# Two attention blocks on one Trainium2 core: a later place in the queues for exponentials and divisions, and an output tile begun inside the last stick-breaking pair

## The chip, the cores and the metric

The kernel runs on one core of one Trainium2 chip. The metric is the device time of one execution in microseconds (us). The core has five engines that each work through a queue of their own in program order: TensorE (PE in the profile, its weight loads PEld), VectorE (DVE), ScalarE (ACT), GpSimd (POOL) and SyncE (SP). They meet only at semaphores: an instruction carries `then_inc`, and another engine's queue stops at `wait_ge`.

## The reference, cut to what matters

The program is two transformer blocks one after the other, on 1024 positions of width 1024, in float32. The change touches two places.

The sparse attention of the first block: every query picks 256 keys by an index score, and six heads in two groups attend to those. The kernel computes full logits and masks them.

```
logits = jnp.einsum('bqgrd,bqkgd->bqgrk', qg, k_sel).astype(jnp.float32) * att_scale
logits = jnp.where(valid[:, :, None, None, :], logits, -jnp.inf)
p = jax.nn.softmax(logits, axis=-1).astype(v.dtype)
o = jnp.einsum('bqgrk,bqkgd->bqgrd', p, v_sel)
```

The stick-breaking attention of the second block (12 heads of 64) and the projection that follows it:

```
log_stay = jnp.where(strict, jax.nn.log_sigmoid(-z), 0.0)
later = lax.cumsum(log_stay, axis=3, reverse=True) - log_stay
w = jnp.where(strict, jnp.exp(jax.nn.log_sigmoid(z) + later), 0.0)
...
y = jnp.concatenate([mix, mem_out.astype(mix.dtype)], axis=-1) @ w_out[layer]
x = layer_norm(DN_ALPHA * x + y, ln_mix_g[layer], ln_mix_b[layer])
```

## The kernel before

Everything stands in one program with the order of every engine's work written out by hand. A float32 product is made of three TensorE passes: each operand is split into a rounded high part and a low part (the difference), and high*high, high*low and low*high are added. So each weight tile of 128x1024 is split by GpSimd (`split`, L467 the high part, L469 the low part) into `w_hi` and `w_lo`, two slots each, and the split of tile t waits until tile t-2 has been used (`tile_done` at t-1). A tile of the big products is 8 blocks of 6 matmuls of 512 columns (L558, L559, L562), and writes one of the two slots of the PSUM tensor `dense`.

The sparse attention. `DSA_PLAN` lists 16 pairs (query block i of 128, group g), called s. Each has 3 heads, so that n = 3s+j counts 48 strips of logits of width 128(i+1). `DSA_TURNS` lists, for each s, its i+1 key blocks: 72 steps x. At step x TensorE turns three 128x128 pieces of the probabilities (`att_turn`, L870), may make logits for a later n (`att_logits`, L858 and L859; `LOGITS_AT` says at which x), and multiplies with the values of step x-2 (`att_values`, L880). The logits of s are made during the steps of s-2, and their turn comes two s later. ScalarE at step x copies the turned piece to SBUF (L1301); then rounds the queries of a later s, where `QUERIES_AT` says so (L1232, once for each s); then takes the exponentials (L1288) of the strips whose logits are made at this same x. VectorE at step x takes the low part of those queries (`split_queries`, L1775, which waits for the rounding), turns the index score into a mask when a new i begins (L1834), adds the mask to the logits and finds the extreme of each row (`mask`, L1839), and divides the strips of step x-1 (`normalise`, L1846 and L1848). TensorE may turn piece x only when the copy of piece x-2 has been made; it may make logits n only when `mask` of n-2 is done.

The stick-breaking attention. 12 heads of 12 steps n (144 in all), two heads are a pair of 24 steps. At step n TensorE makes scores (L1004 to L1006), turns the weights of step n-6 (`turn_weights`, L1016) and multiplies those of step n-8 with the values (`values`, L1030 and L1031), and in all pairs but the last adds a piece of the next pair's projections (L978 to L980). ScalarE takes two sigmoids (L1473, L1479) and rounds the turned weights (L1487). VectorE scans the row (L2060; in the third kind of step a one-column product, L2059, stands before it), and takes the low part of the turned weights (L2067). GpSimd multiplies weights and scan (`stick_steps`, L517) and, at 12 steps of a pair, splits a half of a weight tile (L500, L507). In the last pair (steps 120 to 143) the finished attention output `y2_f` is prepared for the projection: at the steps of `EARLY_AT` (130, 132, ... 142) ScalarE rounds one of 7 blocks of it (L1501) and VectorE takes its low part (`low`, L1638). The eighth block is finished only after the last step.

After the last step TensorE waits for the last head (`y_copied`) and runs `two_tiles`: output tiles `T_OUT2` and `T_OUT2+1` woven together, the second four blocks behind the first. GpSimd splits the weights of `T_OUT2+2` when the first of these two is done. VectorE adds each finished tile to the residual (L2089).

Of the kernel before, what the change touches and what calls it, by code (L numbers as in the profile page):

```python
# [20 lines left out]
F32 = mybir.dt.float32  # L21
F32R = mybir.dt.float32r
ACT = mybir.ActivationFunctionType
ALU = mybir.AluOpType
# [5 lines left out]
KB = D // P  # L30
# [8 lines left out]
SB_H = 12  # L39
# [40 lines left out]
U_OUT2 = U_SB  # L80
# [71 lines left out]
EARLY = 7  # L152
EARLY_AT = {PAIR_STEPS * (SB_H // 2 - 1) + 10 + 2 * j: j for j in range(EARLY)}

# [49 lines left out]
def build(nc, io, out):  # L204
    with ExitStack() as ctx:
# [5 lines left out]
        def sem(name):  # L211
            return ctx.enter_context(nc.semaphore(name))
# [74 lines left out]
        def par(name, k=0):  # L287
# [36 lines left out]
            "h", "mem", "ym", "yc", "ya", "merged", "h2", "hidden", "x2", "mem2", "y2", "x3", "hidden2")}  # L324
        yc_ready = sem("conv_out_ready")

        turned, roped, turn_free = sem("proj_turned"), sem("proj_rotated"), pair("turn_free")
# [136 lines left out]
        def _(pool):  # L464
# [48 lines left out]
            def stick_steps():  # L513
                for n in range(STICK_STEPS):
# [4 lines left out]
                    if n in SPLIT_W:  # L519
                        t, part = SPLIT_W[n]  # L520
                        split_part(T_SB + t, part)

            split_tiles(RAW, T_ATT + 2)
# [18 lines left out]
        def _(pe):  # L542
# [496 lines left out]
            for n in range(STICK_STEPS + PV_LAG):  # L1039
# [9 lines left out]
                if n in TURN_V:  # L1049
                    turn_values(*TURN_V[n])  # L1050

            pe.wait_ge(v_split, SB_H)
            pe.wait_ge(y_copied, 2 * SB_H)
            for n in range(KB):
                if n == 0:
                    two_tiles(T_OUT2, U_OUT2, parts["y2"][1], Y2_ORDER)
                elif 2 <= n < KB - 2:
                    tile(T_OUT2 + n, U_OUT2 + n)
            last_two(3, T_OUT2 + KB - 2, U_OUT2 + KB - 2, lambda h: moments(3, h, U_OUT2))
# [26 lines left out]
        def _(act):  # L1086
# [209 lines left out]
            for x in range(len(DSA_TURNS) + DSA_LAG + 1):  # L1296
# [7 lines left out]
                if x in QUERIES_AT:  # L1304
                    round_queries(QUERIES_AT[x])
                for n in LOGITS_AT.get(x, ()):
                    exponentials(n)
# [249 lines left out]
        def _(dve):  # L1557
# [292 lines left out]
            for n in range(REP * DSA_LEAD + 2):  # L1850
                if n < REP * DSA_LEAD:
                    mask(n)
                if n >= 2:
                    normalise(n - 2)
            for x in range(len(DSA_TURNS)):
                if x in QUERIES_AT:
                    split_queries(QUERIES_AT[x])
                for n in LOGITS_AT.get(x, ()):
                    mask(n)
                for n in LOGITS_AT.get(x - 1, ()):  # L1860
                    normalise(n)

# [180 lines left out]
            for n in range(STICK_STEPS + PV_LAG + 1):  # L2043
# [31 lines left out]
                if n in EARLY_AT:  # L2075
                    j = EARLY_AT[n]
                    k = Y2_ORDER[j]
                    low((a_hi[:, k, :], a_lo[:, k, :]), k, y2_f[:, k, :], "y2", j + 1)

# [274 lines left out]
```

## Time and profile before

| | us |
|---|---|
| median of the timed runs (3) | 3115.48 (3112.72 to 3116.6) |
| the profiled execution, its own time | 3111.55 |
| its span in the profile | 3109.8 |
| sparse attention, first logits to last low part | about 726 to 868 |
| stick-breaking attention, last pair and tail | about 2200 to 2256.5 |
| the two woven output tiles | 2256.55 to 2278.41 |

The page counts busy time by engine over the span: PE 93%, PEld 75%, DVE 54%, ACT 25%, POOL 37%. Its 40 slices are 77.7 us each; the sparse attention lies in slices 10 and 11 and the end of the stick-breaking attention in slices 28 to 30. Averages over the span say little of either place: both are short, and each has its own limit.

### The profile page before, as it was taken

To read this page: it belongs to the slowest core of one execution; us is meant where nothing else is said; L and a number is where in the kernel's file an instruction comes from. 1 tells how busy PE (TensorE), PEld (TensorE's weight loads), DVE (VectorE), ACT (ScalarE), POOL (GpSimd) and SP (SyncE) were. 2 spreads that over 40 slices of the span, in tenths; PEclk is the share of its full clock that TensorE was granted. 3 is DMA by queue.
4 is the path that set the end of the run, shared out by engine and by line. 5 is a ranking of instruction groups with operands and counts; after the bars stand their busy time and mean duration, and the time that the engine had idled before them with its cause. 6 is when DMAs were issued, how large, how long until landed. Compare 5 with 4: busy or idle time off the path is not lost.

```text
span 3109.8 us, 34850 instructions
## 1 busy us (share of the span) xinstructions
PE 2907.6 (93%) x13074; PEld 2347.0 (75%) x13074; DVE 1689.6 (54%) x2299; ACT 789.0 (25%) x1441; POOL 1160.1 (37%) x649
## 2 busy tenths in 40 slices
PE   7987999998899999999999889999798999999997
PEld 5675878886577788888888668878585888888885
DVE  3475899987554423233232638888846233333327
ACT  4055011114622201011020456666613000000003
POOL 2330334442033334333333416555432344433331
PEclk9978999998999999999999999999898999999998
DMA  3110122221051111111111110000020111111111
GB/s 146 41 34 7 48 68 77 79 81 61 1 190 41 41 48 48 47 48 53 47 47 48 62 74 28 21 28 26 16 95 28 48 48 47 47 47 53 48 47 61
DMA packets 45051, 165.37 MB, mean 53 GB/s; under 512 B 4880, under 2 KB 6160, under 8 KB 43920
## 3 DMA queue, kind: packets, MB, share of 16 engines
q1 hardware_dynamic: 37168, 129.31, 12.5%
q10 hardware_dynamic: 7776, 34.61, 2.9%
q8 instruction: 70, 1.15, 0.2%
q14 instruction: 37, 0.30, 0.0%
HBM read 147.12 MB, written 16.78 MB: 53 GB/s over the span
## 4 chain that ended last, share of the span: by engine, by line
PE 80%; DVE 12%; ACT 3%; issue 3%; DVEq 1%; DMA 0%; POOL 0%; ACTq 0%; SPq 0%; POOLq 0%
PE dense L558 21%; PE dense L559 21%; PE dense L562 21%; DVE stay L2060 2%; DVE a_lo L1638 2%; PE dense L978 2%; PE dense L979 2%; PE dense L980 2%; PE dense L598 1%; PE dense L599 1%; PE dense L600 1%; PE side L1016 1%; ACT T L1198 1%; PE side L1005 1%; DVE T L1617 1%
## 5 line engine op out<-in xcount | busy, mean ns | idle before, releaser
L467 POOL TENSOR_TENSOR w_hi<-raw,zero 128x1024 fp32r<-128x1024 f32 x210 | 400.8, 1909 | 1565.6 <-PE dense L562 1298.7
L558 PE MATMUL dense<-a_hi,w_hi 128*128 128x512 f32 x2000 | 783.6, 392 | 14.1 <-DVE T L1791 5.6
L559 PE MATMUL dense<-a_lo,w_hi 128*128 128x512 f32 x2000 | 780.3, 390 | 0.0
L562 PE MATMUL dense<-a_hi,w_lo 128*128 128x512 f32 x2000 | 617.5, 390 | 0.0
L469 POOL TENSOR_TENSOR w_lo<-raw,w_hi 128x1024 fp32r<-128x1024 f32 x210 | 526.1, 2505 | 16.5
L558 PEld LDWEIGHTS dense<-a_hi,w_hi 128*128 128x128 f32 x2000 | 377.0, 188 | 95.8 <-issue 7.7
L559 PEld LDWEIGHTS dense<-a_lo,w_hi 128*128 128x128 f32 x2000 | 376.8, 188 | 79.2 <-issue 1.2
L562 PEld LDWEIGHTS dense<-a_hi,w_lo 128*128 128x128 f32 x2000 | 376.6, 188 | 78.5
L558 PE MATMUL dense<-b_hi,w_hi 128*128 128x512 f32 x832 | 327.2, 393 | 5.2 <-DVE T L1966 2.5
L559 PE MATMUL dense<-b_lo,w_hi 128*128 128x512 f32 x832 | 324.7, 390 | 0.0
L1946 DVE TENSOR_TENSOR x_res<-x_res,dense 128x1024 f32<-128x1024 f32 x100 | 122.0, 1220 | 329.6 <-PE dense L562 328.3
L1966 DVE SCALAR_TENSOR_TENSOR T<-dense,tiny,T 128x1023 f32<-128x1023 f32 x88 | 112.9, 1282 | 296.3 <-ACT T L1370 293.0
L562 PE MATMUL dense<-b_hi,w_lo 128*128 128x512 f32 x832 | 256.8, 390 | 0.0
L517 POOL TENSOR_TENSOR stick_weights<-stick_weights,stay 128x511 f32<-128x511 f32 (+2 forms) x144 | 132.2, 919 | 174.6 <-DVE stay L2060 174.6
L558 PEld LDWEIGHTS dense<-b_hi,w_hi 128*128 128x128 f32 x832 | 156.7, 188 | 45.7 <-issue 4.8
L1530 ACT ACTIVATE b_hi<-T 128x1024 fp32r<-128x1024 f32 x32 | 34.0, 1062 | 610.7 <-DVE T L2139 610.7
L562 PEld LDWEIGHTS dense<-b_hi,w_lo 128*128 128x128 f32 x832 | 156.5, 188 | 32.9
L559 PEld LDWEIGHTS dense<-b_lo,w_hi 128*128 128x128 f32 x832 | 156.8, 188 | 31.9
L1370 ACT ACTIVATE T<-dense,tiny 128x1024 f32<-128x1024 f32 x44 | 49.2, 1117 | 516.9 <-PE dense L562 511.1
L1742 DVE MATCH_REPLACE8 score<-tiny,score 128x384 f32<-128x384 f32 (+2 forms) x192 | 165.7, 876 | 0.0
L1738 DVE MAX8 tiny<-score 128x8 f32<-128x384 f32 (+2 forms) x192 | 155.4, 877 | 2.9 <-issue 1.6
L2137 DVE TENSOR_SCALAR T<-dense 128x1024 f32<-128x1024 f32 x32 | 39.2, 1225 | 192.1 <-PE dense L562 190.5
(277 smaller groups left out, 4360.0 us busy)
## 6 DMA issues: line engine op xcount, KB each, us to landing
raw<-in_w_stream SPq DMA_DIRECT2D x231, 512.0 KB, 3.3
x_in<-in_x_t SPq DMA_DIRECT2D x8, 512.0 KB, 7.4
spill_gate<-T ACTq DMA_DIRECT2D x8, 512.0 KB, 2.6
spill_part<-gates ACTq DMA_DIRECT2D x8, 512.0 KB, 2.6
back<-spill_gate ACTq DMA_DIRECT2D x8, 512.0 KB, 3.7
back<-spill_part ACTq DMA_DIRECT2D x8, 512.0 KB, 4.6
x_res<-in_x_t ACTq DMA_DIRECT2D x2, 2048.0 KB, 9.0
spill_x<-x_res ACTq DMA_DIRECT2D x1, 4096.0 KB, 13.4
```

Source lines behind the costliest of these rows:

```text
L467: pool.tensor_tensor(w_hi[:, r % 2, :], raw[:, r, :], zero[:, 0:1].broadcast_to([P, D]), ALU.add).then_inc(weights_rounded, 1)
L469: pool.tensor_tensor(w_lo[:, r % 2, :], raw[:, r, :], w_hi[:, r % 2, :].bitcast(F32), ALU.subtract).then_inc(weights_split, 1)
L517: pool.tensor_tensor(w[:, 0:width - 1], w[:, 0:width - 1], stay[n % STRIPS][:, 1:width], ALU.mult).then_inc(w_ready, 1)
L558: pe.matmul(o, w_hi[:, slot, w], hi[:, k, x], start=b == 0, stop=False)
L559: pe.matmul(o, w_hi[:, slot, w], lo[:, k, x], start=False, stop=False)
L562: last = pe.matmul(o, w_lo[:, slot, w], hi[:, k, x], start=False, stop=stop)
L978: pe.matmul(o, w_hi[:, t % 2, w], a_hi[:, b, x], start=b == 0, stop=False)
L979: pe.matmul(o, w_hi[:, t % 2, w], a_lo[:, b, x], start=False, stop=False)
L1738: dve.max(best[:, i - TOPK // P, :], score[:, score_at(i):score_at(i + 1)])
L1742: dve.match_replace(sc, best[:, i - TOPK // P, :], sc, TAKEN)
L1946: dve.tensor_tensor(x_res[:, n, :], x_res[:, n, :], dense[:, u % 2, :], ALU.add).then_inc(sums_free[u % 2], 1)
L1966: last = dve.scalar_tensor_tensor(T[:, slot, d:S], dense[:, u % 2, 0:S - d], tap, T[:, slot, d:S], ALU.mult, ALU.add)
```

## The change

In the sparse attention, ScalarE takes the exponentials one step later (those of x-1 at step x, behind the copy and the rounding of x). VectorE's step becomes: mask, divide the strips of x-2 (before x-1), and last the low part of the queries (before: first).

In the last stick-breaking pair, the 7 early blocks of `y2_f` are rounded three steps earlier (steps 127, 129, ... 139). The low parts of blocks j = 0, 2, 4, 6 move from VectorE to GpSimd; VectorE keeps 1, 3 and 5. Nine steps after each, TensorE multiplies the block for the output tile `T_OUT2+1` (at steps 136, 138, ... 148). After the last head, TensorE runs 7 blocks of tile `T_OUT2`, and then the eighth block of both.

```diff
-EARLY_AT = {PAIR_STEPS * (SB_H // 2 - 1) + 10 + 2 * j: j for j in range(EARLY)}
+EARLY_AT = {PAIR_STEPS * (SB_H // 2 - 1) + 7 + 2 * j: j for j in range(EARLY)}
+FIRST_AT = {n + 9: j for n, j in EARLY_AT.items()}
...
# GpSimd, stick_steps
+                    if n in EARLY_AT and EARLY_AT[n] % 2 == 0:
+                        j, k = EARLY_AT[n], Y2_ORDER[EARLY_AT[n]]
+                        pool.wait_ge(parts["y2"][0], j + 1)
+                        pool.tensor_tensor(a_lo[:, k, :], y2_f[:, k, :], a_hi[:, k, :].bitcast(F32), ALU.subtract
+                                           ).then_inc(y2_low, 1)
...
# TensorE, loop over the stick-breaking steps and what follows
-
-            pe.wait_ge(v_split, SB_H)
+                if n in FIRST_AT:
+                    j = FIRST_AT[n]
+                    if j == 0:
+                        pe.wait_ge(v_split, SB_H)
+                        pe.wait_ge(weights_split, T_OUT2 + 2)
+                    pe.wait_ge(parts["y2"][1] if j % 2 else y2_low, j // 2 + 1)
+                    product((T_OUT2 + 1) % 2, halves(dense, (U_OUT2 + 1) % 2), a_hi, a_lo, j + 1, begin=j, end=False, order=Y2_ORDER)
+
             pe.wait_ge(y_copied, 2 * SB_H)
-            for n in range(KB):
-                if n == 0:
-                    two_tiles(T_OUT2, U_OUT2, parts["y2"][1], Y2_ORDER)
-                elif 2 <= n < KB - 2:
-                    tile(T_OUT2 + n, U_OUT2 + n)
+            product(T_OUT2 % 2, halves(dense, U_OUT2 % 2), a_hi, a_lo, EARLY, end=False, order=Y2_ORDER)
+            pe.wait_ge(parts["y2"][1], KB // 2)
+            for n in range(2):
+                product((T_OUT2 + n) % 2, halves(dense, (U_OUT2 + n) % 2), a_hi, a_lo, KB, begin=EARLY, order=Y2_ORDER
+                        ).then_inc(tile_done, 1)
+            for n in range(2, KB - 2):
+                tile(T_OUT2 + n, U_OUT2 + n)
...
# ScalarE, sparse attention
-                for n in LOGITS_AT.get(x, ()):
+                for n in LOGITS_AT.get(x - 1, ()):
                     exponentials(n)
...
# VectorE, sparse attention
             for x in range(len(DSA_TURNS)):
+                for n in LOGITS_AT.get(x, ()):
+                    mask(n)
+                for n in LOGITS_AT.get(x - 2, ()):
+                    normalise(n)
                 if x in QUERIES_AT:
                     split_queries(QUERIES_AT[x])
-                for n in LOGITS_AT.get(x, ()):
-                    mask(n)
-                for n in LOGITS_AT.get(x - 1, ()):
-                    normalise(n)
...
# VectorE, stick-breaking
-                    low((a_hi[:, k, :], a_lo[:, k, :]), k, y2_f[:, k, :], "y2", j + 1)
+                    if j % 2:
+                        low((a_hi[:, k, :], a_lo[:, k, :]), k, y2_f[:, k, :], "y2", j + 1)
```

## Rows read from the trace of the kernel before

**Rows 1.** The page: span.

```profile
span 3109.8 us, 34850 instructions
```

**Rows 2.** Busy time by stretch: us, PE, PEld, DVE, ACT, POOL, PEclk (granted clock), DMA.

```profile
737.20:763.90 26.70, 21.56 (x91) 15.27 (x89) 17.53 (x61) 19.06 (x50) 2.02 (x2) 0.84 0.22 80
763.90:837.30 73.40, 58.21 (x263) 39.41 (x262) 42.18 (x95) 43.97 (x95) 4.01 (x4) 0.93 0.00 1
```

**Rows 3.** Waits from 763.9 to 837.3: who waited for whom, us, times, longest.

```profile
ACT strip L1288 <- DVE tiny L1839: 28.2, 18, 2.8
...
PE dense L870 <- ACT att_probs_t L1301: 15.2, 9, 3.2
DVE qq L1775 <- ACT qq L1232: 14.6, 7, 3.0
```

**Rows 4.** Timeline around step 29: start, us, engine, line, operation, idle before.

```profile
799.26 0.52 ACT L1232 ACTIVATE qq<-q_f 64x384 fp32r<-64x384 f32 x1
...
799.81 0.56 DVE L1775 SCALAR_TENSOR_TENSOR qq<-q_f,qq 64x384 fp32r<-64x384 f32 x1 [2.02 <-ACT qq L1232]
...
801.21 1.09 DVE L1839 CUSTOM_DVE_ANT_0 strip<-side,score 128x896 f32<-128x896 f32 x1 [0.18 <-issue]
...
802.34 1.04 ACT L1288 ACTIVATE strip<-strip,tiny 128x896 f32<-128x896 f32 x1 [2.56 <-DVE tiny L1839]
...
803.29 0.18 ACT L1288 ACTIVATION_READ_ACCUMULATOR strip<-strip,tiny 128x1 f32 x1
...
803.91 0.47 PE L870 MATMUL dense<-ident,strip 128*128 128x128 f32 x1 [2.60 <-ACT att_probs_t L1301]
```

**Rows 5.** Timeline of ACT where no logits are left: first and last of 11 copies.

```profile
854.01 0.49 ACT L1301 ACTIVATE att_probs_t<-dense 128x384 f32<-128x384 f32 x1 [0.47 <-PE dense L870]
...
863.76 0.49 ACT L1301 ACTIVATE att_probs_t<-dense 128x384 f32<-128x384 f32 x1 [0.48 <-PE dense L870]
```

**Rows 6.** Timeline of PE: turns before and after one strip, 640 and 1024 wide.

```profile
769.45 0.49 PE L870 MATMUL dense<-ident,strip 128*128 128x128 f32 x3
...
771.11 0.49 PE L870 MATMUL dense<-ident,strip 128*128 128x128 f32 x3
...
835.86 0.49 PE L870 MATMUL dense<-ident,strip 128*128 128x128 f32 x3
...
837.76 0.49 PE L870 MATMUL dense<-ident,strip 128*128 128x128 f32 x3
```

**Rows 7.** Busy time by stretch: last pair from scan 128 to 143; the two tiles.

```profile
2204.20:2244.80 40.60, 22.66 (x106) 17.71 (x106) 40.57 (x52) 26.84 (x55) 19.19 (x18) 0.78 0.04 14
2256.50:2278.40 21.90, 21.85 (x96) 18.13 (x97) 2.45 (x2) 2.12 (x2) 4.30 (x2) 1.00 0.52 204
```

**Rows 8.** Timeline of DVE: scan 128 alone, scan 130 beside a GpSimd pass.

```profile
2203.05 1.28 DVE L2060 TENSOR_TENSOR_SCAN stay<-stay,stay,zero 128x512 f32<-128x512 f32 x1
...
2208.81 2.38 DVE L2060 TENSOR_TENSOR_SCAN stay<-stay,stay,zero 128x512 f32<-128x512 f32 x1
```

**Rows 9.** Timeline of POOL: the passes beside scan 130; a whole weight split.

```profile
2207.79 1.09 POOL L517 TENSOR_TENSOR stick_weights<-stick_weights,stay 128x511 f32<-128x511 f32 x1 [1.29 <-DVE stay L2060]
2208.83 1.28 POOL L507 TENSOR_TENSOR w_lo<-raw,w_hi 128x512 fp32r<-128x512 f32 x1
...
2271.86 1.90 POOL L467 TENSOR_TENSOR w_hi<-raw,zero 128x1024 fp32r<-128x1024 f32 x1 [25.94 <-PE dense L562]
2273.83 2.40 POOL L469 TENSOR_TENSOR w_lo<-raw,w_hi 128x1024 fp32r<-128x1024 f32 x1
```

**Rows 10.** Groups of DVE from 2200 to 2250: busy us, mean ns; the eighth low part.

```profile
L1638 DVE TENSOR_TENSOR a_lo<-y_f,a_hi 128x1024 fp32r<-128x1024 f32 x7 | 11.8, 1690 | 0.0
...
2258.44 1.23 DVE L1638 TENSOR_TENSOR a_lo<-y_f,a_hi 128x1024 fp32r<-128x1024 f32 x1 [1.99 <-ACT a_hi L1507]
```

**Rows 11.** Timeline of PE: first product of the two tiles; first of the third.

```profile
2256.55 0.47 PE L558 MATMUL dense<-a_hi,w_hi 128*128 128x512 f32 x1 [1.45 <-issue]
...
2278.41 0.39 PE L558 MATMUL dense<-a_hi,w_hi 128*128 128x512 f32 x1
```

More of the change, by code:

```diff
@@ L325, in build @@
         yc_ready = sem("conv_out_ready")
+        y2_low = sem("y2_split_by_pool")
         turned, roped, turn_free = sem("proj_turned"), sem("proj_rotated"), pair("turn_free")
```

## The prediction

> **What bounds the kernel now.** I first read the page: the span is 3109.8 us [rows 1], and TensorE is busy for most of it, so a change counts only where TensorE stands idle or runs at the lower clock. Two stretches of the timeline belong to the change, and I read each by busy time, then by waits, then row by row.
>
> The sparse attention. From step 11 (its low part of the queries, L1775, starts at 763.9) to step 48 (its mask starts at 837.3) TensorE is busy for 58.2 of 73.4 us and its granted clock is 0.93, so a part of it ran at 1.2 GHz instead of 2.4 [rows 2]. The list of waits gives all of the 15.2 us of idleness to one wait: TensorE's turn (L870) waits for ScalarE's copy (L1301). ScalarE in its turn stood 28.2 us before its exponentials, waiting for VectorE's mask, and VectorE stood 14.6 us waiting for the rounded queries of ScalarE [rows 3]. Around step 29 the chain can be read link by link: ScalarE rounds the queries at 799.26, VectorE takes their low part at 799.81, then masks at 801.21, ScalarE's exponentials start at 802.34 after 2.56 us of idleness, its copies come behind, and TensorE's next turn starts at 803.91 after 2.60 us [rows 4]. The copies that TensorE wants are queued behind an exponential that is not ready.
>
> What would be left without these waits: a bare step lasts 9.75/10 = 0.975 us, from eleven copies in the tail of the stage [rows 5]. One strip of logits adds 1.66 - 0.975 = 0.69 us where it is 640 wide and 1.90 - 0.975 = 0.93 us where it is 1024 wide [rows 6]; for the 21 strips of steps 11 to 47, of 640 to 1024, I take the middle, 0.80. That makes 37 x 0.975 + 21 x 0.80 = 52.9 us for TensorE at its full clock. The stretch has 73.4, so 20.5 us are to be had: 15.2 of waiting, and 5 of lower clock, which agrees with 7% of 73.4.
>
> The end of the stick-breaking attention. From scan 128 to scan 143 VectorE is busy for 40.57 of 40.6 us [rows 7]: it is the bound, and TensorE has 18 us of room at a granted clock of 0.78. Then the two woven output tiles keep TensorE full for 21.86 us [rows 7, 11].
>
> **The change part by part: sparse attention.** Nothing is added or removed here, only the order changes. (1) ScalarE copies x+1 before it takes the exponentials of x, so the mask (1.09 us) has a whole step to finish; the wait of 28.2 us mostly goes. (2) VectorE masks before it waits for the queries, so L1775 and the ScalarE rounding leave the chain: 0.52 + 0.56 us and the mask of the score at each of the 12 rounds. (3) The division comes one step later. It is wanted only about one s later (4 steps or more from s = 6 on), so I cost it at nothing; what hides it is the lead of two s of the logits. (4) `split_queries` is now queued behind a mask and up to three divisions; TensorE wants it at the first strip of the next s, 4 to 6 steps on, but only 1 to 3 steps on before step 11. No DMA moves past anything: ScalarE's two fetches keep their place ahead of the exponentials.
>
> What is late next: not VectorE (42.2 us busy in 73.4) nor ScalarE (44.0), both under TensorE's 52.9 [rows 2]. But ScalarE at 44.0 of 52.9 is 83% full, and an exponential with its accumulator read (1.04 + 0.18 us, [rows 4]) still stands between two copies, so some waits remain. I take 16 of the 20.5 us, bounds 7 and 20. For steps 1 to 11 (737.2 to 763.9) TensorE is idle for 5.1 of 26.7 us at clock 0.84 [rows 2]; VectorE has many short strips there and becomes the bound, and (4) works against the gain: I take 2, bounds -3 and 6. For steps 48 to 54 I take 1. Sum: 19 us.
>
> **The change part by part: last stick-breaking pair.** (a) VectorE loses four low parts. In place they lasted 1.69 us on average, alone 1.23 [rows 10]; the difference is waiting for GpSimd, which the next scan would have to do as well. So VectorE is relieved of 4 x 1.2 = 4.8 us.
>
> (b) GpSimd gets four passes of the same kind as L469 over 1024 columns: 2.40 us each [rows 9], 9.6 us in all, and GpSimd has 21 us of room there [rows 7]. But the room is not what counts. Scan 128 lasts 1.28 us with GpSimd still; scan 130 lasts 2.38 us [rows 8], and in the second GpSimd's low-part pass began at 2208.83 and ended at 2210.11 [rows 9]: 2210.11 + 1.08 = 2211.19 is where the scan ends. The scan, which has its operands in SBUF, waited out the whole GpSimd pass. So the two engines take turns, and every pass moved to GpSimd is time in which VectorE's chain of scans stands still: +9.6. What VectorE does from PSUM (L2067, L2049) can run beneath, but that already runs beneath GpSimd's product L517, which goes first in the queue. So (a) and (b) make the last scan 9.6 - 4.8 = 4.8 us later; I take +5. Bounds: -6.8 (the passes cost VectorE nothing, all four of 1.69 are saved) and +9.6 (nothing is saved).
>
> The Trainium skill, "SBUF — State Buffer", section "SBUF: two separate sides", says the same against this change: the port pair of VectorE and GpSimd is a lock held for a whole instruction, and a VectorE instruction with two SBUF inputs waits for a GpSimd one that reads SBUF. By it the pair gets longer; by VectorE's busy time alone it would get 6.8 us shorter.
>
> (c) ScalarE's seven roundings only move three steps forward; it has 13 us of room [rows 7]. (d) TensorE's seven pieces of tile `T_OUT2+1`, 21.86/16 = 1.37 us each [rows 11], go into the pair. Four of them (steps 136 to 142) fall into gaps that wait for VectorE, and three into the tail, where they stand between turned weights but also keep the clock up (0.78 now); I cost them at nothing, bounds -1.5 and +4. Their operands are nine steps old, and the waits for them end no later than the ones TensorE has at that step anyway.
>
> (e) After the last head, TensorE had 16 pieces before tile `T_OUT2+2`, and now 9: 9.6 us less. (f) But the weights of `T_OUT2+2` may be split only when `T_OUT2` is done. Now this happens when 8 pieces are done, with one piece (1.37 us) left to cover GpSimd's 1.90 + 2.40 + 0.2 = 4.5 us [rows 9]; before, 4 to 5 pieces of the second tile covered it. TensorE stands 3.1 us. The eighth block's low part ends at 2259.67 [rows 10], 3.1 us after the first product, beneath the first seven pieces: nothing. So (e) and (f) give -9.6 + 3.1 = -6.5.
>
> Sum of the place: +5 - 6.5 = -1.5 us. Over both places: -19 - 1.5 = -20.5. The profiled execution took 3111.55 us, 1.75 more than its span, and would take 3091; the median of the runs lies 3.9 above it, so I predict 3115.5 - 20.5 = 3095.
>
> **The rivals.** (R1) ScalarE becomes the limit at every strip: an exponential, its read and a copy, 1.04 + 0.18 + 0.49 = 1.7 us [rows 4, 5], against a step of 0.975, and TensorE's one turn of lead doesn't absorb it. Then 21 x 0.73 = 15 us of the 20.5 stay, the stage gives 5.5 + 2, and with the other place the time is 3106.5. For it: ScalarE is second busiest. Against: only 21 of 37 steps have a strip.
>
> (R2) VectorE doesn't wait for the moved passes, as they fall where it waits anyway. Then the last scan comes 6.8 us earlier and the place gives 13.3: 3083. Against: 40.57 of 40.6 us busy.
>
> (R3) R1, and the inserted pieces lie on the path: 7 x 1.37 = 9.6 us, so that (e) is void and (f) and +5 remain. -7.5 + 5 + 3.1 = +0.6: 3116.
>
> (R4, slower) The low part of the queries at the end of VectorE's step. If TensorE reaches the first strip of the next s before VectorE reaches that line, it stands through mask, division and low part, 1.09 + 0.9 + 0.56 = 2.5 us, at each of 12 rounds: +30, against 19, with -1.5: 3125. It decides from the point where VectorE runs behind TensorE by the distance between rounds; with the distances of 4 to 6 steps it doesn't, with those of 1 to 3 (five rounds, +12.5) it may, but that alone leaves a gain.
>
> **How the numbers follow.** Forecast 60%, R1 17%, R2 11%, R3 8%, R4 4%. The forecast's own range is 3088 to 3103 (16 may be 10 to 19, +5 may be 2 to 9). To leave out no more than 2 in 10 it is widened to R1 and R2's edge: 3084 to 3107. A measurement of this kernel can tell 0.2%, 6.2 us, from no change. Faster by more: forecast, R1, R2, 88%; within: R3, 8%; slower: R4, 4%.
>
> **What would show it.** Right: ScalarE's wait before L1288 falls from 28.2 to under 8 us in the same steps, TensorE's wait for L1301 from 15.2 to under 5, the granted clock rises to 1.0, and steps 11 to 48 last 57 us. In the pair, GpSimd's low parts last 2.4 to 3.5 us, scans beside them over 2 us, the last head ends some 5 us later counted from step 128, and TensorE stands about 3 us before tile `T_OUT2+2`. Wrong: a wait of TensorE for L1775 (R4), scans as long as before (R2), or the sparse stage shorter by less than 10 us (R1).

## The result, and the profile after

The changed kernel takes 3081.96 us (median of 4 runs, 3080.82 to 3083.52); the kernel before, timed beside it, 3116.04. The ratio is 0.9893 with the interval 0.9876 to 0.991: 34.1 us less, where 20.5 were forecast. The time lies 2 us below the range, whose lower end was 3084. The profiled executions are 29.5 us apart, 3111.55 and 3082.01; below it is said how much of the difference between 34.1 and 29.5 has a cause that the traces show.

The changed lines bear new numbers in the profile after: the exponential L1288 is now L1303, the copy L1301 is L1316, TensorE's turn L870 is L877, the mask L1839 is L1854, the division L1846 and L1848 are L1861 and L1863, the queries' low part L1775 is L1790, the scan L2060 is L2075, GpSimd's weight split L467 and L469 is L469 and L471, the products L558, L559 and L562 are L565, L566 and L569. New is GpSimd's low part, L527. In the kernels of the experiments these numbers can be a few lines off.

First the page of after, its span and TensorE's share, beside [rows 1]:

```profile
span 3080.2 us, 34848 instructions
## 1 busy us (share of the span) xinstructions
PE 2901.3 (94%) x13074; PEld 2345.6 (76%) x13074; DVE 1690.0 (55%) x2295; ACT 788.6 (26%) x1441; POOL 1174.0 (38%) x653
```

**The sparse attention.** Stretches are best cut at ScalarE's copies, one for each of the 72 steps, since these have the same number in every kernel. The busy time by stretch, with the columns of [rows 2], from the copy of step 0 to that of step 11 and from there to that of step 48; before, then after:

```profile
734.52:762.82 28.30, 21.37 (x85) 14.99 (x85) 19.67 (x69) 19.56 (x54) 2.02 (x2) 0.80 0.21 75
762.82:837.83 75.01, 59.82 (x271) 40.52 (x270) 42.71 (x96) 45.51 (x100) 4.01 (x4) 0.93 0.00 1
```

```profile
736.03:757.90 21.87, 19.80 (x85) 14.00 (x85) 18.72 (x67) 18.75 (x51) 2.02 (x2) 0.83 0.28 97
757.90:809.06 51.16, 51.16 (x265) 37.46 (x264) 43.26 (x97) 44.67 (x101) 4.21 (x4) 1.00 0.00 1
```

In steps 11 to 48 TensorE is busy for all of 51.16 us, at a granted clock of 1.00. Its own busy time fell too, from 59.82 us, for the same products. A part of that is clock: a granted clock of 0.93 over 75.01 us means that some of the matmuls ran at 1.2 GHz, and 0.07 x 75.01 = 5.3 us is my estimate of the most that it can have cost. The rest comes with the waits themselves, as a kernel below shows that has waits at the full clock. Steps 0 to 11 lost 6.4 us, steps 11 to 48 lost 23.85, and the 23 steps behind them 0.7 (25.93 and 25.20). That is 31.0 us. What is left of the waits of [rows 3], in the same steps of after (who waits for whom, us, times, longest):

```profile
...
ACT att_probs_t L1316 <- PE dense L877: 5.6, 9, 1.4
DVE strip L1854 <- PE side L866: 2.5, 6, 0.8
DVE tiny L1861 <- ACT strip L1303: 2.3, 3, 1.4
PEld dense L877 <- ACT att_probs_t L1316: 1.2, 3, 0.5
...
ACT strip L1303 <- DVE tiny L1854: 0.3, 2, 0.2
```

ScalarE's 28.2 us before its exponentials are 0.3, and TensorE's 15.2 us before its turns are gone; only its weight load still waits 1.2 us, without holding up a matmul. Among TensorE, ScalarE and VectorE the largest wait now goes the other way: ScalarE waits for TensorE. The same place as [rows 4], around step 29, read from the timeline of after (start, us, engine, line, operation, idle before):

```profile
781.73 0.96 DVE L1854 CUSTOM_DVE_ANT_0 strip<-side,score 128x768 f32<-128x768 f32 x1 [0.54 <-PE side L866]
...
782.17 0.49 PE L877 MATMUL dense<-ident,strip 128*128 128x128 f32 x3
...
782.70 0.49 ACT L1316 ACTIVATE att_probs_t<-dense 128x384 f32<-128x384 f32 x1 [0.48 <-PE dense L877]
...
783.76 0.94 ACT L1303 ACTIVATE strip<-strip,tiny 128x768 f32<-128x768 f32 x1
783.97 0.49 PE L877 MATMUL dense<-ident,strip 128*128 128x128 f32 x3
...
784.18 1.09 DVE L1854 CUSTOM_DVE_ANT_0 strip<-side,score 128x896 f32<-128x896 f32 x1 [0.18 <-issue]
...
784.94 0.49 PE L877 MATMUL dense<-ident,strip 128*128 128x128 f32 x3
...
785.32 1.04 ACT L1303 ACTIVATE strip<-strip,tiny 128x896 f32<-128x896 f32 x1 [0.15 <-DVE tiny L1854]
```

The exponential over 768 columns starts at 783.76 right behind ScalarE's earlier work; its mask had started at 781.73 and lasted 0.96 us, so it was done 1.1 us earlier; the turns follow one another at 1.80 us with a strip between (782.17 to 783.97) and at 0.97 us without (784.94).

**The last stick-breaking pair.** Here moments are told from the start of the first scan of the whole stage, 1866.75 before and 1837.21 after. "The last value" is the start of VectorE's last sum into `y_f` (L2049, now L2064), which the output tiles wait for. Scan 128 started at 336.30 before and at 338.61 after, scan 143 at 376.73 and 377.77, the last value came at 389.01 and 390.99 and the third output tile (`T_OUT2+2`) at 411.66 and 410.27. So the pair itself became 2.0 us longer and the products behind it 3.4 us shorter. After, at the first moved low part, GpSimd and then VectorE:

```profile
2173.51 2.36 POOL L527 TENSOR_TENSOR a_lo<-y_f,a_hi 128x1024 fp32r<-128x1024 f32 x1
```

```profile
2174.41 1.48 DVE L2074 TENSOR_TENSOR stick_weights<-stick_weights,stay 128x1 f32<-128x1 f32 x1 [0.42 <-ACT stay L1494]
2175.82 1.27 DVE L2075 TENSOR_TENSOR_SCAN stay<-stay,stay,zero 128x512 f32<-128x512 f32 x1
```

VectorE's product of a single column lasts 1.48 us, and it ends at 2175.89, when GpSimd's pass does (2173.51 + 2.36 = 2175.87). The last pass of the four does the same at the product before a later scan (1.86 us). Scan 128 is 2.3 us later than before. But that is not the price of GpSimd's pass. The same place in the kernel whose low parts are all on VectorE (below), where the product has no pass of GpSimd beside it:

```profile
2173.54 1.96 DVE L1648 TENSOR_TENSOR a_lo<-y_f,a_hi 128x1024 fp32r<-128x1024 f32 x1 [0.30 <-ACT a_hi L1511]
...
2176.25 0.16 DVE L2069 TENSOR_TENSOR stick_weights<-stick_weights,stay 128x1 f32<-128x1 f32 x1
2176.33 1.28 DVE L2070 TENSOR_TENSOR_SCAN stay<-stay,stay,zero 128x512 f32<-128x512 f32 x1
```

Here the product lasts 0.16 us, but VectorE's own low part stands ahead of it, and scan 128 starts at 338.24, only 0.4 us earlier than with GpSimd. So 1.9 of the 2.3 us come from taking the first low part three steps earlier, ahead of scan 128, on whichever engine.

TensorE behind the last value, and at the third tile:

```profile
2228.94 0.79 PE L565 MATMUL dense<-a_hi,w_hi 128*128 128x512 f32 x1 [1.40 <-DVE y_f L2064]
...
2247.48 0.47 PE L565 MATMUL dense<-a_hi,w_hi 128*128 128x512 f32 x1 [3.19 <-POOL w_lo L471]
```

and the busy time of the first 6 us behind the one gap and the first 10 behind the other:

```profile
2228.90:2234.90 6.00, 5.96 (x14) 4.71 (x15) 1.22 (x1) 1.06 (x1) 0.00 (x0) 0.50 0.90 351
2247.50:2257.50 10.00, 10.00 (x37) 8.10 (x38) 0.91 (x1) 0.00 (x0) 5.03 (x2) 0.83 0.33 107
```

In both the granted clock is at the lower level for some or all of the time: TensorE does 14 matmuls in 6 us, and 27 in the kernel that closes the gap (below). Here each gap costs twice, as idleness and as clock. The first gap is not new: it was 1.45 us long before [rows 11]. The second is.

### The profile page after: what moved, and what is told of

It is laid out like the page before. It is cut to its first block, busy times and chain, and to the rows that moved or that the text cites. A ratio compares the mean times of both kernels' runs of the same rounds, so it can differ in the third digit from the quotient of the medians.

```text
span 3080.2 us, 34848 instructions
## 1 busy us (share of the span) xinstructions
PE 2901.3 (94%) x13074; PEld 2345.6 (76%) x13074; DVE 1690.0 (55%) x2295; ACT 788.6 (26%) x1441; POOL 1174.0 (38%) x653
## 4 chain that ended last, share of the span: by engine, by line
PE 82%; DVE 11%; ACT 2%; issue 2%; POOL 1%; DVEq 1%; DMA 0%; ACTq 0%; SPq 0%; POOLq 0%
PE dense L565 21%; PE dense L566 21%; PE dense L569 21%; PE dense L985 2%; PE dense L986 2%; PE dense L987 2%; DVE stay L2075 2%; DVE a_lo L1653 2%; PE dense L605 1%; PE dense L606 1%; PE dense L607 1%; PE dense L887 1%; PE side L1023 1%; ACT T L1213 1%; PE side L1012 1%
## 5 line engine op out<-in xcount | busy, mean ns | idle before, releaser
L469 POOL TENSOR_TENSOR w_hi<-raw,zero 128x1024 fp32r<-128x1024 f32 x210 | 401.3, 1911 | 1565.8 <-PE dense L569 1298.3
L565 PE MATMUL dense<-a_hi,w_hi 128*128 128x512 f32 x2000 | 785.1, 393 | 17.2 <-DVE T L1806 5.6
L566 PE MATMUL dense<-a_lo,w_hi 128*128 128x512 f32 x2000 | 781.6, 391 | 0.0
L569 PE MATMUL dense<-a_hi,w_lo 128*128 128x512 f32 x2000 | 618.4, 391 | 0.0
L471 POOL TENSOR_TENSOR w_lo<-raw,w_hi 128x1024 fp32r<-128x1024 f32 x210 | 525.0, 2500 | 16.5
L565 PEld LDWEIGHTS dense<-a_hi,w_hi 128*128 128x128 f32 x2000 | 377.5, 189 | 99.6 <-issue 9.4
L566 PEld LDWEIGHTS dense<-a_lo,w_hi 128*128 128x128 f32 x2000 | 377.5, 189 | 79.0 <-issue 1.2
L569 PEld LDWEIGHTS dense<-a_hi,w_lo 128*128 128x128 f32 x2000 | 377.3, 189 | 79.2
L565 PE MATMUL dense<-b_hi,w_hi 128*128 128x512 f32 x832 | 327.2, 393 | 5.2 <-DVE T L1981 2.5
L566 PE MATMUL dense<-b_lo,w_hi 128*128 128x512 f32 x832 | 324.7, 390 | 0.0
L569 PE MATMUL dense<-b_hi,w_lo 128*128 128x512 f32 x832 | 256.7, 390 | 0.0
L565 PEld LDWEIGHTS dense<-b_hi,w_hi 128*128 128x128 f32 x832 | 156.7, 188 | 45.8 <-issue 4.9
L569 PEld LDWEIGHTS dense<-b_hi,w_lo 128*128 128x128 f32 x832 | 156.5, 188 | 32.9
L566 PEld LDWEIGHTS dense<-b_lo,w_hi 128*128 128x128 f32 x832 | 156.8, 188 | 31.7
```

The source lines that it names most:

```text
L469: pool.tensor_tensor(w_hi[:, r % 2, :], raw[:, r, :], zero[:, 0:1].broadcast_to([P, D]), ALU.add).then_inc(weights_rounded, 1)
L471: pool.tensor_tensor(w_lo[:, r % 2, :], raw[:, r, :], w_hi[:, r % 2, :].bitcast(F32), ALU.subtract).then_inc(weights_split, 1)
L565: pe.matmul(o, w_hi[:, slot, w], hi[:, k, x], start=b == 0, stop=False)
L566: pe.matmul(o, w_hi[:, slot, w], lo[:, k, x], start=False, stop=False)
L569: last = pe.matmul(o, w_lo[:, slot, w], hi[:, k, x], start=False, stop=stop)
```

## The experiments

Times are medians; "before" is always the kernel before, timed beside the kernel in question on the same chip. The kernels came in three groups, and before took 3115.91, 3115.2 and 3114.66 us in them (3116.04 beside the changed kernel), so a difference between kernels of different groups is uncertain by a microsecond or so.

**The two places apart.** The diff shown ahead of the prediction is cut in two. The first kernel has only this of it, and the old pair; the second has all the rest.

```diff
-                for n in LOGITS_AT.get(x, ()):
+                for n in LOGITS_AT.get(x - 1, ()):
                     exponentials(n)
...
+                for n in LOGITS_AT.get(x, ()):
+                    mask(n)
+                for n in LOGITS_AT.get(x - 2, ()):
+                    normalise(n)
                 if x in QUERIES_AT:
                     split_queries(QUERIES_AT[x])
```

> Only the order in the sparse attention is changed, the last stick-breaking pair is as before. Theory S (the whole gain of 34 us lies in the sparse attention, as the ledger of the two traces has it: 31 us there, 1.5 us of drift elsewhere): 3085 us, 30 to 32 below the kernel before. Rival (the sparse part is worth the 19 us that I forecast, and the rest comes from the pair): 3097 us.

Measured: 3084.88 us, ratio 0.9901 (0.9885 to 0.9918): -31.0 us, as the first theory has it. Steps 11 to 48 last 51.15 us, as in the changed kernel.

> Only the last stick-breaking pair and the output tiles are changed, the sparse attention is as before. Theory S: 0 to 2 us below the kernel before, since the head ends 2 us later, the tiles start 9.6 us shorter, and GpSimd's split and the lower clock take 3 us each. Rival: 12 to 15 us below.

Measured: 3111.46 us, ratio 0.9988 (0.9978 to 0.9997): -4.4 us. That is more than the 0 to 2 us expected, though the interval (0.9 to 6.9 us) reaches into them. Together the two kernels gain 35.4, beside the 34.1 of the whole change. So nine tenths come from the sparse attention, and the pair gains a little more than forecast, though its trace looks like a draw. The traces say in part why. From the first scan to the end of the span it is 1243.0 to 1243.1 us in all three kernels with the new pair and the early products (the changed one, the pair alone, and the changed one with doubled masks, below). With the old pair the profiled execution of before has 1243.0, but the five other kernels with the old pair have 1245.4 to 1245.5. They part behind the last value. Busy time of 7 us from there, of the kernel with the old pair and the new orders:

```profile
2223.70:2230.70 7.00, 6.98 (x24) 5.57 (x25) 1.23 (x1) 1.06 (x1) 0.00 (x0) 0.76 0.93 359
```

The granted clock is at 0.76 here, and in the other four as well, where it was 1.00 in the profiled execution of before [rows 7]. That execution was a favourable one; against the usual one the new pair is worth 2.5 us.

This explains a part of the difference between the two figures of the result. The profiled executions differ by 31.0 - 1.5 = 29.5: the three parts of the sparse attention gave 31.0, and the stage began 1.5 us later (its first copy at 736.03 and not 734.52; over the executions of all kernels that copy comes between 734.4 and 737.7). The medians differ by 4.5 us more, of which 2.5 are the favourable execution of before. The other 2 us are not explained. From the last copy of the sparse attention to the first scan, a stretch that no edit touches, the profiled executions take between 1000 and 1003.6 us, so a remainder of this size can't be given to any part of the change.

**Which order does it.** The first kernel moves only the exponentials, the second only the split of the queries, behind mask and division, and the third exponentials and divisions but not the split.

```diff
-                for n in LOGITS_AT.get(x, ()):
+                for n in LOGITS_AT.get(x - 1, ()):
                     exponentials(n)
```

> Only ScalarE's exponentials come one step later; VectorE keeps its old order. Theory Q (the round trip of the queries, ScalarE's rounding to VectorE's low part to the mask, is most of the wait): 8 to 14 us below the kernel before, since VectorE still waits for the rounding before it masks, but the exponentials no longer stand in front of the copy. Rival E (the place of the exponentials is all that counts): 27 us or more below.

```diff
-                if x in QUERIES_AT:
-                    split_queries(QUERIES_AT[x])
                 for n in LOGITS_AT.get(x, ()):
                     mask(n)
                 for n in LOGITS_AT.get(x - 1, ()):
                     normalise(n)
+                if x in QUERIES_AT:
+                    split_queries(QUERIES_AT[x])
```

> Only VectorE's order is changed: mask, then the division of the step before, then the low part of the queries; ScalarE keeps its old place for the exponentials. Theory Q: 8 to 14 us below the kernel before, as the query round trip leaves the chain, but every exponential still stands before the next copy and waits 1 us or more for its mask. Rival E: 3 us or less below.

```diff
-                for n in LOGITS_AT.get(x, ()):
+                for n in LOGITS_AT.get(x - 1, ()):
                     exponentials(n)
...
-                for n in LOGITS_AT.get(x - 1, ()):
+                for n in LOGITS_AT.get(x - 2, ()):
                     normalise(n)
```

> The kernel before with exponentials and divisions one step later, the split of the queries still ahead of the mask on VectorE; the stick-breaking pair is as before. With the exponentials alone later the 37 steps 11 to 48 took 56.5 us, with all three orders changed 51.2. If what is left there is the split's wait for ScalarE, which the mask behind it on VectorE inherits: 56 us again, 3090 to 3091 us. If it is the division that waits for an exponential issued in the same step: 51 to 52 us, 3085 to 3086 us.

Measured, with the parts of the stage in us:

| orders changed | time | less than before beside it | steps 0 to 11 | 11 to 48 | 48 to 71 |
|---|---|---|---|---|---|
| none | 3115.91 | | 28.30 | 75.01 | 25.93 |
| split last | 3094.85 | 21.1 | 23.61 | 59.92 | 25.93 |
| exponentials later | 3090.93 | 25.0 | 25.27 | 56.48 | 25.19 |
| exponentials and divisions later | 3088.37 | 26.3 | 25.55 | 53.25 | 25.20 |
| all three | 3084.88 | 31.0 | 21.42 | 51.15 | 25.21 |

Neither theory of the first two was right (8 to 14 us each, or 27 or more and 3 or less). The two edits don't halve the gain between them, nor does one have it all: each alone brings most of it, as both cut the same chain (queries rounded, their low part, mask, exponential, copy). With one link out, what is left fits nearly into a step. The waits of steps 11 to 48 with the split last:

```profile
ACT strip L1288 <- DVE tiny L1839: 13.6, 14, 1.7
...
PE dense L870 <- ACT att_probs_t L1301: 4.4, 6, 1.6
DVE qq L1775 <- ACT qq L1232: 1.2, 1, 1.2
```

and its busy time:

```profile
760.73:820.65 59.92, 55.34 (x271) 37.23 (x270) 42.47 (x96) 45.30 (x101) 4.01 (x4) 1.00 0.00 1
```

The granted clock of that stretch is 1.00, not 0.93, and yet TensorE is busy for 55.34 us, 4.2 more than in the changed kernel, for the same products. So with waits between the matmuls the trace counts more busy time at the full clock too, and of the 8.7 us that TensorE's busy time fell by (59.82 to 51.16) at most 4.5 are the clock's. With the exponentials later alone it is 9.0, 3.3 and 3.1 us for these, and 1.00 as well. The clock thus came back to 1.00 with either edit, before the waits were gone. The third kernel tells the rest apart. Taken in this order, the later division is worth 3.2 us in steps 11 to 48 (56.48 to 53.25), the split's place 2.1 more, and in steps 0 to 11 it is the split's place that counts, 25.55 to 21.42 (21.4 to 22.7 in all seven executions with these orders and no doubled mask). Its 53.25 us lie between what I gave for the one cause and for the other; both have a share, the division the larger.

**How much room the new order has.** Every fourth mask is done twice, in the changed kernel and in the one before.

```diff
+                if n % 4 == 1:
+                    dve.tensor_tensor_reduce(out=strip_of(n), ...)
+                    dve.drain()
                 dve.tensor_tensor_reduce(out=strip_of(n), ...)
```

> The changed kernel with every fourth mask of the sparse attention done twice on VectorE, about 1.0 us more work each time, five times in steps 11 to 48 and some more before. Slack theory (with the new order TensorE alone sets these steps, and VectorE's 43 of 51 us are off the path): steps 11 to 48 stay within 1 us of 51.2, and the time within 2 us of 3082. Chain theory (mask, exponential and division still follow one another within what a step lasts): 4 to 6 us more in these steps, 3087 to 3090 us.

> The kernel before with the same every fourth mask done twice. Chain theory for the order before (mask, exponential, its division and the next mask lie in one row, so that work on VectorE goes straight to the end): 4 to 6 us more in the 37 steps 11 to 48 than 75.0, and 3121 to 3124 us in all. If VectorE's waits there absorb it: 3116 us.

Measured: 3088.89 us (0.9916, 0.9899 to 0.9933), 6.9 over the changed kernel; and 3124.98 (1.0029, 1.0019 to 1.0038), 10.3 over before. VectorE's busy time over steps 0 to 71 rose by 8.4 us in both. In steps 11 to 48 it rose by 3.8 us in the new kernel (43.26 to 47.05) and the stretch by 3.3, to 54.48; in the old one by 5.0 and 5.5, to 80.54. My slack theory, with at most 1 us, falls. The chain theory had 4 to 6 us in these steps: in the new order it is a little less, and in the old one the time is 1 us above the 3121 to 3124 expected, with executions from 3118.5 to 3126.5. TensorE was full in these steps but the chain of mask, exponential and division stood right behind it: its waits are back at once, here those of steps 11 to 48 with the doubled masks in the new order.

```profile
ACT strip L1303 <- DVE tiny L1858: 6.4, 8, 1.7
...
PE dense L877 <- ACT att_probs_t L1316: 1.3, 2, 1.1
```

**The price of GpSimd's low parts.** All seven on VectorE, the rest as changed.

```diff
-                    pool.tensor_tensor(a_lo[:, k, :], y2_f[:, k, :], a_hi[:, k, :].bitcast(F32), ALU.subtract
-                                           ).then_inc(y2_low, 1)
...
# TensorE, for each early piece
-                    pe.wait_ge(parts["y2"][1] if j % 2 else y2_low, j // 2 + 1)
+                    pe.wait_ge(parts["y2"][1], j + 1)
...
-                    if j % 2:
-                        low((a_hi[:, k, :], a_lo[:, k, :]), k, y2_f[:, k, :], "y2", j + 1)
+                    low((a_hi[:, k, :], a_lo[:, k, :]), k, y2_f[:, k, :], "y2", j + 1)
```

> The changed kernel with all seven low parts of the output's input on VectorE, as before the change; the early products and the sparse attention's orders stay. Port theory (each GpSimd pass over 128x1024 numbers holds VectorE's scans for its whole 2.4 to 3.3 us, where VectorE's own pass takes 1.2): from the start of the stick-breaking attention to the end of scan 143 about 2 us less than in the changed kernel (whose scan 143 comes 1.9 us later than before), so 3080 us. Relief theory (four passes taken from VectorE are 4.8 us of its time saved): scan 143 later by up to 4.8 us, 3085 to 3087 us. If the head is bound by something else than VectorE: 3082 us, as the changed kernel.

Measured: 3082.11 us (0.9892, 0.9875 to 0.9908), by time the same as the changed kernel, where 3080 was expected. By the trace, scan 143 starts at 376.46 and the last value comes at 389.66, both 1.3 us earlier than in the changed kernel; in the six profiled kernels with the new pair and GpSimd's low parts scan 143 lies between 377.7 and 378.3. The relief theory is out: taking four passes of VectorE's away didn't shorten its chain, it lengthened it. The size is smaller than the forecast's 4.8, and the time alone couldn't have shown it; another pair of kernels does, below. The third tile starts 2.6 us earlier than in the changed kernel, but what follows it lasts 1.5 us longer, with the same granted clock of 0.83 in the first 10 us; why is not shown.

**The price of the early products.** Low parts on GpSimd, but both tiles multiplied after the last value.

```diff
-                if n in FIRST_AT:
-                    ...
-                    product(..., j + 1, begin=j, end=False, order=Y2_ORDER)
...
+            two_tiles(T_OUT2, U_OUT2, None, Y2_ORDER)
```

> The changed kernel with the four low parts on GpSimd, but both output tiles multiplied after the last values, as before the change. What it prices is moving seven of sixteen pieces of 1.36 us each ahead. Full theory (the move is worth its 9.5 us): 3091 us. Clock and stall theory (in the changed kernel the move is worth 9.5 us less 3.0 us for the granted clock of 0.50 after the gap of 1.4 us, and less 3.2 us for the stall ahead of the third tile, which comes with it): 3085 us, the granted clock in the first 10 us after the last values 1.00, and the stall ahead of the third tile under 1 us. Nothing theory (the products inserted in the pair cost the head what they save behind it): 3082 us.

Measured: 3083.46 us (0.9896, 0.988 to 0.9913; 3081.20 to 3087.53), 1.5 us over the changed kernel, where 3085 was expected. The executions spread over 6 us, and the profiled one is the longest, so its end proves little. Its moments do: the last value comes at 390.16, 0.8 us earlier than with the inserted products, and the third tile at 414.2, 3.9 us later. The 9.6 us of products moved ahead are thus worth 3.9 at that point. The granted clock behind the last value is 0.75, not the 1.00 I expected; there is no stall before the third tile, as expected.

**The gap behind the last value.** The seventh early piece is held back until the last product of the values is issued, so it fills TensorE's wait of 1.4 us.

```diff
-FIRST_AT = {n + 9: j for n, j in EARLY_AT.items()}
+FIRST_AT = {n + 9: j for n, j in EARLY_AT.items() if j < EARLY - 1}
...
+            pe.wait_ge(y2_low, 4)
+            product((T_OUT2 + 1) % 2, ..., EARLY, begin=EARLY - 1, end=False, order=Y2_ORDER)
             pe.wait_ge(y_copied, 2 * SB_H)
```

> The changed kernel with one of the seven early pieces (the seventh) multiplied after the last product of the values, where TensorE waits 1.4 us for VectorE's last values, instead of two steps earlier. Clock theory (the granted clock falls to 0.50 because TensorE stands still in that gap): idle time ahead of the next product under 0.5 us, the clock 1.00 behind it, 3.0 us less: 3079 us. Rival (the clock falls by what TensorE did in the head before, sparse work with waits, so one piece more or less in the gap doesn't change it): clock 0.50 in the next 6 us still, 3082 us; the piece's own time is off the path only in the first case and in the second it saves nothing, since the gap's end is set by VectorE.

Measured: 3080.0 us (0.9888, 0.9872 to 0.9905; 3079.52 to 3080.85), 2.0 us less than the changed kernel and 1 us above the 3079 expected; the changed kernel's fastest execution was 3080.82. The firmer evidence is the trace. Busy time of the 6 us behind the end of the last value, to be read beside the row at 2228.90 above:

```profile
2228.10:2234.10 6.00, 5.97 (x27) 4.96 (x27) 1.23 (x1) 1.06 (x1) 0.00 (x0) 1.00 0.84 326
```

The clock stays at 1.00, and 27 matmuls run in place of 14. The third tile starts at 406.96, 3.3 us earlier, as the clock theory says. Only 1.7 of it reach the end. The stall before the third tile is 3.19 us as ever, and in the 10 us behind it the clock is now 0.69, against 0.83, which would be 1.4 us. That what was saved at one gap was in part paid at the next fits these rows, but isn't shown: with the low parts on VectorE the same 1.5 us go behind the third tile at a clock of 0.83.

**The stall before the third tile.** The two tiles change places, so the tile whose weight slot the third one needs is done five pieces before the other. The seventh piece stays held back. Besides what is shown, the first two weight tiles are fetched in the other order, and VectorE's first sum of an output tile waits for both.

```diff
-            product(T_OUT2 % 2, ..., EARLY, end=False, order=Y2_ORDER)
+            product((T_OUT2 + 1) % 2, ..., 3, end=False, order=Y2_ORDER)
...
+            product(T_OUT2 % 2, ..., KB, begin=EARLY, order=Y2_ORDER).then_inc(tile_done, 1)
+            product((T_OUT2 + 1) % 2, ..., KB, begin=3, order=Y2_ORDER).then_inc(tile_done, 1)
```

> As the kernel with the seventh piece held back, and the two first output tiles change places: the tile begun early is the one whose weights lie in the slot that the third tile needs, it is finished five pieces before the other, and GpSimd's two passes for the third tile (1.9 and 2.4 us) start that much earlier. Stall theory (the 3.2 us ahead of the third tile are GpSimd's passes, begun at the last use of the slot): the stall falls to the 1.4 us or so that the eviction of the sums needs, 1.8 us less than that kernel, and up to 1.7 us more if the granted clock (0.74 behind the stall) stays at 1.00: 3075.5 to 3077 us beside 3079. Rival (the stall is hidden anyway by what follows, since the tiles' evictions by VectorE at 2.5 us each or the transfers of weights set the pace): no difference to that kernel.

Measured: 3076.78 us (0.9878, 0.9862 to 0.9895; 3076.76 to 3077.51), 3.2 less than with the piece held back and within the 3075.5 to 3077 of the stall theory. The third tile's start:

```profile
2242.20 0.50 PE L565 MATMUL dense<-a_hi,w_hi 128*128 128x512 f32 x1 [1.38 <-DVE x_res L2107]
```

The stall is 1.38 us, now for VectorE's eviction of the sums, and the clock behind it stays at 1.00. GpSimd's passes did set the 3.2 us, which is also what the profile names as ending that wait (`POOL w_lo L471`, above).

**Both together with the low parts back on VectorE.** The edits are those of the kernel with the tiles swapped and of the one with the low parts on VectorE.

> As the kernel with the two first output tiles in the other order, and all seven low parts of the output's input on VectorE. Port theory (from the kernel with the low parts on VectorE alone: scan and last values 1.3 us earlier than in the changed kernel): the last values come 1.3 us earlier after the start of the stick-breaking attention than with the tiles swapped alone (391.0 us there), and the time is 3075.5 us. Rival (the products of the low parts wait longer on VectorE's queue, and the early pieces move behind the last values): 3077 to 3080 us.

Measured: 3073.61 us (0.9867, 0.9851 to 0.9884; 3073.04 to 3074.03), 3.2 less again, 1.9 below the 3075.5 expected, and the fastest of all, 8.4 below the changed kernel. The last value comes at 389.18, 1.8 us earlier than with the tiles swapped alone. In both kernels the executions lie within 1 us of one another, so this is the firmest measure of (a) with (b): to give GpSimd four of the low parts costs 1.8 us at the last value and 1.9 at the third tile. The other 1.4 us arise behind the third tile, where the two kernels have the same program, and can't be put down to the low parts.

## Why the prediction was off

The direction was right, and so were the mechanisms in the main: the waits of the sparse attention, VectorE's waiting for GpSimd, and the stall before the third tile. The size was too small by 13.6 us. By its steps:

The largest term was mis-sized. The floor of 52.9 us for TensorE was sound: measured are 51.2 us, 1.7 less. But I took 16 of the 20.5 us above it, "so some waits remain", with ScalarE 83% full. None of TensorE's remained. ScalarE is at 44.67 of 51.16, 87%, and no matmul of TensorE waits for a copy. Besides, my cut from 763.9 to 837.3 left out 1.6 us that the same 37 steps have when they are cut at the copies, 75.0 and not 73.4. Taken to the floor: 16 + 4.5 (the rest of the 20.5) + 1.6 + 1.7 = 23.8, which is the 23.85 measured. So 7.9 of the missing 13.6 us lie here.

Steps 1 to 11 gave 6.4 us, a little over the upper bound of 6 and not the 2 I took. The step that failed is (4), that the late split would work against the gain there. It did the opposite: the split's place alone carries 2.8 to 4.1 us of it (25.55 without it, 21.4 to 22.7 with it; 21.87 in the changed kernel). As in the later steps, the split was waiting for ScalarE with the mask behind it. With that 12.3 us are explained. Steps 48 and on gave 0.7 for 1.

The pair was forecast at -1.5 and is worth 0 against the profiled execution and -2.5 against the usual one (-4.4 with an interval from -6.9 to -0.9 by time). That it came near the forecast is luck, since inside it errors cancel:
- (a) and (b): +4.8 forecast, +1.3 and +1.8 measured in two pairs of kernels. That VectorE stands still beside GpSimd's pass is right, down to one column; the rule that the prediction cites from the Trainium skill, "SBUF — State Buffer", "SBUF: two separate sides", agrees with the 1.48 us of that row. But adding up 9.6 us of passes less 4.8 of relief overstates it: the first pass costs 0.4 us at scan 128 and the other three 0.9 by scan 143, against the kernel with all low parts on VectorE. For one thing, VectorE's own low part waits there as well, 1.96 us for the 1.23 that it takes alone.
- (d): inserted products at nothing, 0.8 us measured at the last value. That they "keep the clock up" was true before the gap (0.97 in the last 13 us, 0.72 in the old pair), but no use behind it.
- (e): the 9.6 us less of products left out the clock behind the gap of 1.4 us, 3 us by the kernel that closes it. The usual execution of the old pair pays 1.7 us there too, so it is a full 3 us only against the profiled execution. (f) was right, 3.19 us for 3.1, but the clock behind that stall was left out as well (0.83 in 10 us, some 1.7 us).

The rivals: R1 and R3 are out, since no matmul waits for a copy any more. R4 is out by its price: the list of waits of steps 0 to 71 has no wait of VectorE for the queries, and of TensorE for their low part one of 0.5 us, in steps 0 to 11. R2 named 3083, near the time measured, by a mechanism that the row of 1.48 us and the run with the low parts on VectorE contradict: the last scan comes 1.0 us later than before, not 6.8 earlier. Of what I said would show the forecast right, the waits, the clock of 1.00, GpSimd's 2.4 to 3.5 us and the stall came as told; 51 us and not 57, and 2 us and not 5, are the two sizes that missed. Scans of over 2 us beside the moved passes did not come: what waited there were the one-column products (1.48 and 1.86 us) and a low part of VectorE's (2.74), while the two scans of 2.1 us stand in the kernel with all low parts on VectorE too.

Open is why a stretch behind the last value is granted the full clock in the profiled execution of before and not in five others with the same pair, and what makes the program behind the third tile last from 831.3 to 834.4 us in one kernel and another.

## What to carry over

When two engines' waits form one ring (round, split, mask, exponential, copy), its gain isn't a share of the wait. One link taken out brought 15 or 18.5 of the 23.9 us of steps 11 to 48, and with all three orders changed the stretch fell to the floor of the fullest engine, clock included. Forecast the floor, and count a discount only for a wait that can be named. Then look at the room: here there was next to none, and 1 us more of work on VectorE cost 0.8 to 0.9 us again.

Work brought forward from behind a wait empties what followed it. Before crediting the whole of it, look at the gaps that stand there and what the clock does behind them: one small piece kept back for a gap, and the order of two tiles turned round, were worth 5 us with no work removed. And compare more than one profiled execution before giving 2 or 3 us to a cause.

## What the hardware showed

A wait of 1.40 us of TensorE, after 13 us at a granted clock of 0.97, was followed by 0.50 (1.2 GHz) for 6 us in the changed kernel and in the kernel with the new pair alone, and after 13 us at 1.00 by 0.72 with the low parts on VectorE; with that wait filled by one piece of six matmuls it was 1.00. A wait of 1.45 us, after 13 us at 0.72 or 0.73, was followed by 1.00 in the profiled execution of before and by 0.72 in five other kernels with the same pair. Behind the stall of 3.19 us the clock was 0.83 (four kernels) and 0.69 (the one with the piece held back) in 10 us, and behind the one of 1.38 it was 1.00. So a gap of about one and a half microseconds can be followed by the lower clock, and need not be.

A VectorE product over a single column in SBUF waited out GpSimd's pass, 1.48 us for 0.16. GpSimd's low part over 1024 columns lasted 2.36 and 2.39 us, but 3.01 and 3.31 us where a scan of VectorE was under way when it began: 2.77 on average, where I had reckoned with 2.40.
